# Down-projection weights loaded as one 16 KB run per partition, in a mixture-of-experts decoder kernel

## The chip, the core and the metric

The kernel runs on one core of a Trainium2 chip. The metric is the device time of one execution in microseconds (us). TensorE multiplies matrices (PE in the profile, its weight loads PEld), VectorE is DVE, ScalarE is ACT, GpSimd is POOL, and SyncE (SP) only issues DMA transfers here. SBUF is the memory on the chip with 128 partitions; HBM is the memory outside it.

## The reference, cut to what matters

Two decoder layers over 256 tokens of width 1024, all in fp32: in each an attention mixer with a residual add, then a mixture of experts with a residual add, and a final RMSNorm. The attention parts are not touched here. The expert part is, for each layer:

```
grp = top-1 of 4 groups;  top-2 of the 8 experts in that group       # per token
hid = silu(xb @ w_gate[e]) * (xb @ w_up[e])    # w_gate, w_up: 1024 x 512
y   = hid @ w_down[e]                          # w_down: 512 x 1024
out[token] += y * gate_weight
```

There are 32 experts in a layer. Each of the three matrices of an expert is 2 MiB, so the experts of one layer are 201 MB of weights, nearly all that the kernel reads.

## The kernel before, in words

The order of work is written out by hand for each engine, with semaphores between them. A layer is: projection of the attention inputs, attention, output product, routing, experts.

**Experts.** Every expert is computed for up to 32 of its tokens ("slots"). Experts go in groups of three (GE = 3): ten full groups, 0 to 9, and a tail group of two. For a full group TensorE does in turn:

- the gather of the tokens' rows by a product with a one-hot matrix (L835);
- for each of the three experts the gate and up product (L867): the 32 slots are the stationary operand, and the moving one is a piece of 128 gate columns and the same 128 up columns, so 256 columns for each of 8 chunks c of the inner dimension. The hidden dimension of 512 is cut into four pieces j. The pieces lie in four column strips of the array (tile_position), so the result stands in PSUM with piece j at rows 32j to 32j+31;
- the turn of the hidden values (L853), which gives hidT[k] with the place within the piece on the partitions and (piece, slot) along the row;
- keep_warm(6) (L736), products whose result nobody reads, issued after the wait for the second down block and ahead of the wait for the third;
- the down product (L887): for each piece j, the slots of piece j times row block j of the down weights;
- the scatter back to the tokens (L917), added to h by VectorE (L1301).

The profile shows each fp32 matmul as two instructions.

**The ring.** `ring` holds nine blocks of 16 KB per partition: gate and up of expert k at 2k and 2k+1, down at 6+k. Each is used once per group and filled again for the next group. SP issues all loads into one queue, in this order for a group: gate and up of expert k when the gate and up product of expert k of the group before is done (gate_up_done); then, when the down product of the group before is done (down_done), the three down blocks (load_down, L407). The tail group loads its last down block in two column halves (L429). For group 0 the loads are issued during and behind attention.

**Layouts.** Gate and up rows are spread so that partition p has rows 8p to 8p+7: one run of 16 KB in HBM. Down rows j*128+p are on partition p for j = 0 to 3: four runs of 4 KB. Row 128j+p of the down weights thus meets place p of piece j in hidT.

Of the kernel before, what the change touches and what calls it, by code (L numbers as in the profile page):

```python
# [1 line left out]

# [13 lines left out]
P = 128  # L36
# [28 lines left out]
HID = 512  # L65
# [121 lines left out]
def build(nc, x, mix_even, w_in_even, w_out_even, mix_odd, w_in_odd, w_out_odd, ffn_norm,  # L187
# [4 lines left out]
    with ExitStack() as ctx:  # L192
# [18 lines left out]
        ring = sb("ring", [P, 9, UNIT])  # L211
# [92 lines left out]
        e_arrived = [sems(f"e_arrived{l}_", 9) for l in range(LAYERS)]  # L304
# [82 lines left out]
        @block.sync  # L387
        def _(sp):
            gate_rows = w_gate.rearrange("l e (p c) n -> (l e) p (c n)", c=C)
            up_rows = w_up.rearrange("l e (p c) n -> (l e) p (c n)", c=C)  # L390
            down_rows = w_down.rearrange("l e (j p) n -> (l e) p j n", p=P)

            def load_group(l, r, g, experts, first_expert, after_attention=False):
                for k in range(experts):

                    if after_attention:
                        sp.wait_ge(proj_done[l], 2 * T * (k + 1))
                    else:
                        sp.wait_ge(gate_up_done[l], gu_count(r, g, k) - GE)
                    if after_attention and k == experts - 1:  # L400
                        load_w_out(l, 0)
                    row = l * EXPERTS + first_expert + k
                    sp.dma_start(ring[:, 2 * k, :], gate_rows[row]).then_inc(e_arrived[l][2 * k], 16)
                    sp.dma_start(ring[:, 2 * k + 1, :], up_rows[row]).then_inc(e_arrived[l][2 * k + 1], 16)
                def load_down(k):
                    row = l * EXPERTS + first_expert + k
                    sp.dma_start(ring[:, 6 + k, :].rearrange("p (j n) -> p j n", j=HID // P),  # L407
                                 down_rows[row]).then_inc(e_arrived[l][6 + k], 16)

                if after_attention:  # L410

                    sp.wait_ge(s_done[l], n_items[l])
                    load_w_out(l, 1)
                    load_down(2)
                    for k in range(2):
                        sp.wait_ge(mixed[l], T * (k + 1))
                        load_down(k)
                else:
                    sp.wait_ge(down_done[l], down_no(r, g))
                    for k in range(experts):  # L420
                        if experts == GE or k < experts - 1:
                            load_down(k)
                        else:

                            row = l * EXPERTS + first_expert + k
                            slot = ring[:, 6 + k, :].rearrange("p (j n) -> p j n", j=HID // P)
                            for half, arrived in ((0, e_arrived[l][6 + k]), (1, e_arrived[l][7 + k])):
                                cols = slice(512 * half, 512 * half + 512)
                                sp.dma_start(slot[:, :, cols], down_rows[row][:, :, cols]).then_inc(arrived, 16)  # L429

            def load_w_out(l, n):
                sp.dma_start(ring[:, 6 + n, :].rearrange("p (c n) -> p c n", c=C),
                             w_out[l][0].rearrange("(c p) n -> p c n", p=P)[:, :, 512 * n:512 * n + 512])\
                  .then_inc(w_arrived[6 + n], 16)

            def load_round(l, r, after_attention=False):
                if after_attention:
                    load_group(l, r, 0, GE, 0, after_attention)
                with sp.Fori(int(after_attention), FULL) as g:
                    load_group(l, r, g, GE, g * GE)  # L440
                load_group(l, r, FULL, TAIL, FULL * GE)

            for t in range(T):
                sp.dma_start(h[:, t, :], x[0, P * t:P * t + P, :]).then_inc(x_loaded[t], 16)
            sp.dma_start(cst[:, 0:FIRST_CONSTS], consts[:, 0:FIRST_CONSTS]).then_inc(const_loaded[0], 16)

            def load_gain(i, g):
                sp.dma_start(gains[:, i, :], g.rearrange("(p c) -> p c", c=C)).then_inc(gain_loaded[i], 16)

            load_gain(0, mix[0][0])  # L450
            more = None
            for l in range(LAYERS):
                w_in_v = w_in[l][0].rearrange("(p c) n -> p c n", c=C)
                for j in range(NW):
                    if l:

                        sp.wait_ge(gate_up_done[l - 1],
                                   gu_count(more, FULL, j // 2))
                    b = BLOCKS[l][j]
                    block, source = ring[:, j, :].rearrange("p (c n) -> p c n", c=C), w_in_v[:, :, 512 * b:512 * b + 512]  # L460
                    if j == 0:

                        sp.dma_start(block[:, 0:C // 2, :], source[:, 0:C // 2, :]).then_inc(w_begun, 16)
                        sp.dma_start(block[:, C // 2:, :], source[:, C // 2:, :]).then_inc(w_arrived[j], 16)
                        if l == 0:
                            for i, g in ((1, ffn_norm[0]), (2, mix[1][0]), (3, ffn_norm[1])):
                                load_gain(i, g)
                    else:
                        sp.dma_start(block, source).then_inc(w_arrived[j], 16)
                    if l == 0 and j == 2:  # L470
                        sp.dma_start(cst[:, FIRST_CONSTS:], consts[:, FIRST_CONSTS:]).then_inc(const_loaded[1], 16)
                if l == 0:
                    for m in range(LAYERS):
                        for dst, src in ((w_rt[:, m, :, 0:GROUPS], w_group[m].rearrange("(p c) e -> p c e", c=C)),
                                         (w_rt[:, m, :, GROUPS:], w_fine[m].rearrange("(p c) e -> p c e", c=C)),
                                         (b_rt[:, m, 0:GROUPS], b_group[m].partition_broadcast(P)),
                                         (b_rt[:, m, GROUPS:], b_fine[m].partition_broadcast(P))):
                            sp.dma_start(dst, src).then_inc(router_loaded, 16)
                load_round(l, 0, after_attention=True)
                sp.wait_ge(rounds_ready[l], 1)  # L480
                more = sp.value_load(rounds_i[0:1, l:l + 1], min_val=0, max_val=MAX_ROUNDS - 1)
                with sp.If(more > 0):
                    with sp.Fori(1, more + 1) as r:
                        load_round(l, r)

            for t in range(T):
                sp.wait_ge(xn_ready, T * LAYERS + t + 1)
                sp.dma_start(out[0, P * t:P * t + P, :], xn_t[:, t, :]).then_inc(out_stored, 16)
            sp.wait_ge(out_stored, T * 16)
# [242 lines left out]
        def _(pe):  # L732
# [80 lines left out]
            def values(l, a):  # L813
# [11 lines left out]
                                         start=(kt == 0), stop=(kt == T - 1), tile_position=(0, lo))  # L825
                last.then_inc(pair_done[l], 1)

            def experts_of(l, r, g, n):
                no = group_no(r, g)
                rows = SLOTS * n  # L830
# [24 lines left out]
                for k in range(n):  # L855
                    e = expert_no(r, g, k)
                    if k >= 2:
                        pe.wait_ge(gate_up_out[l], e - 1)
                    pe.wait_ge(e_arrived[l][2 * k], arrivals(2 * k, r, g))
                    pe.wait_ge(e_arrived[l][2 * k + 1], arrivals(2 * k + 1, r, g))  # L860
                    bank = psum[2 + k % 2]

                    for c in range(C):
                        if k == 0 and c == C // 2:
                            pe.wait_ge(xT_ready[l], no * 2 + 2)
                        for j in range(4):
                            last = pe.matmul(  # L867
                                bank[32 * j:32 * j + 32, 0:2 * P].rearrange("p (a s) -> p a s", a=2),
                                xT[:, c, SLOTS * k:SLOTS * k + SLOTS],
                                ring[:, 2 * k:2 * k + 2, 512 * c + P * j:512 * c + P * j + P],  # L870
                                start=(c == 0), stop=(c == C - 1), tile_position=(0, 32 * j))

                    last.then_inc(gate_up_done[l], 1 if n == GE or k < n - 1 else 1 + GE - n)
                    if k:
                        turn_hid(k - 1)
# [544 lines left out]
```

## Time and profile before

| | before |
|---|---|
| three runs, us | 1230.98, 1231.55, 1232.72 |
| median, us | 1231.55 |
| span of the profiled execution, us | 1232.3 |
| granted TensorE clock, mean | 0.925 |
| TensorE busy | 1022.5 us (83%) |
| VectorE busy | 421.3 us (34%) |
| ScalarE busy | 208.8 us (17%) |
| DMA, mean over the span | 358 GB/s, 441.25 MB |

The span is that of the one profiled execution, from its first to its last instruction. The page gives no other time of that execution; the span lies within the range of the three runs, so what lies around it is too small to be seen here. Busy time is the share of the span in which an engine has work; TensorE's includes keep_warm.

### The profile page before, as it was taken

The page shows a single profiled execution, that of the slowest core. Times are in us where ns is not written, and L with a number is a line of the kernel's source. Part 1 is how long each engine was busy: PE and PEld are TensorE (multiplying, and loading weights), DVE is VectorE, ACT ScalarE, POOL GpSimd, SP SyncE. Part 2 cuts the span into 40 slices and gives each one's busy share as a digit, 9 for nine tenths or more (in the row PEclk, how much of TensorE's full clock was granted, in tenths as well). Part 3 has the DMA queues.
Part 4 walks back from the last instruction along what each step waited for, and adds up shares of the span by engine and source line. Part 5 has one row for each costly group of instructions (what it writes and reads, how often), then busy time and mean ns, then how long its engine had stood idle before and what let it go on. Part 6 is the DMA issues. An engine that isn't in the chain of part 4 may idle for free.

```text
span 1232.3 us, 18607 instructions
## 1 busy us (share of the span) xinstructions
PE 1022.5 (83%) x7588; PEld 562.9 (46%) x7588; DVE 421.3 (34%) x1031; ACT 208.8 (17%) x531; POOL 36.6 (3%) x52
## 2 busy tenths in 40 slices
PE   8998988797787787787799999896977887877786
PEld 6874534442442442443378656344434433433442
DVE  5774522321321221222278735323212212221313
ACT  5643110100000000000155630001000000000101
POOL 1002000000000000000010210000000000000000
PEclk9999999998998898898889998999988998997988
DMA  9856389999999999999945543999999999999992
GB/s 358 285 212 266 137 343 419 418 430 418 418 427 423 419 423 424 419 421 421 362 165 239 225 168 124 376 419 416 428 422 420 423 425 419 421 426 420 419 421 106
DMA packets 76307, 441.25 MB, mean 358 GB/s; under 512 B 8816, under 2 KB 8816, under 8 KB 59760
## 3 DMA queue, kind: packets, MB, share of 16 engines
q1 hardware_dynamic: 76128, 440.26, 87.6%
q10 hardware_dynamic: 144, 0.52, 0.1%
q8 instruction: 22, 0.36, 0.1%
q14 instruction: 13, 0.11, 0.0%
HBM read 439.72 MB, written 1.05 MB: 358 GB/s over the span
## 4 chain that ended last, share of the span: by engine, by line
PE 51%; DMA 39%; DVE 6%; ACT 2%; issue 1%; SPq 1%; POOL 1%; DVEq 0%; ACTq 0%; POOLq 0%
DMA ring<-in_w_expert_down 38%; PE bank L736 12%; PE bank L887 11%; PE bank L867 5%; PE bank L924 4%; PE bank L759 3%; PE bank L761 3%; PE bank L760 3%; PE bank L835 2%; PE bank L917 2%; PE bank L898 1%; PE bank L957 1%; DMA ring<-in_w_in_even 1%; PE bank L810 1%; DVE work L1098 1%
## 5 line engine op out<-in xcount | busy, mean ns | idle before, releaser
L867 PE MATMUL bank<-ring,work 128*32 128x256 f32 x4096 | 249.6, 403 | 43.6 <-DMA ring<-in_w_expert_up 43.2
L867 PEld LDWEIGHTS bank<-ring,work 128*32 128x32 f32 x4096 | 141.8, 116 | 138.9 <-issue 67.6
L736 PE MATMUL bank<-cst 128*128 128x512 f32 x252 | 156.6, 785 | 42.1 <-DMA ring<-in_w_expert_down 42.1
L887 PE MATMUL bank<-ring,work 128*32 128x512 f32 x960 | 141.3, 594 | 0.0
L1296 DVE COPY work<-bank 96x512 f32<-96x512 f32 (+1 forms) x22 | 15.1, 687 | 350.6 <-PE bank L887 337.5
L736 PEld LDWEIGHTS bank<-cst 128*128 128x128 f32 x252 | 62.0, 256 | 119.3 <-issue 119.3
L835 PE MATMUL bank<-work,xn 128*128 128x96 f32 (+1 forms) x704 | 88.6, 287 | 22.9 <-DVE work L1264 22.9
L835 PEld LDWEIGHTS bank<-work,xn 128*128 128x128 f32 x704 | 84.9, 201 | 41.2 <-DVE work L1264 41.2
L917 PE MATMUL bank<-work 96*128 96x512 f32 (+1 forms) x176 | 85.1, 615 | 15.7 <-ACT work L620 15.7
L1290 DVE TENSOR_SCALAR work<-work 128x128 f32<-128x128 f32 x64 | 14.5, 226 | 224.5 <-ACT work L615 224.5
L887 PEld LDWEIGHTS bank<-ring,work 128*32 128x32 f32 x960 | 37.5, 110 | 100.8 <-issue 100.8
L759 PE MATMUL bank<-split,h_high 128*128 128x512 f32 x192 | 78.7, 410 | 5.6 <-DVE split L1089 4.0
L1089 DVE SCALAR_TENSOR_TENSOR split<-ring,gains,split 128x512 fp32r<-128x512 f32 x96 | 68.3, 749 | 27.9 <-ACT split L644 27.0
L760 PE MATMUL bank<-split,h_low 128*128 128x512 f32 x192 | 76.0, 396 | 0.0
L761 PE MATMUL bank<-split,h_high 128*128 128x512 f32 x192 | 76.0, 396 | 0.0
L1301 DVE TENSOR_TENSOR h<-h,bank 128x512 f32<-128x512 f32 x88 | 60.5, 687 | 39.8 <-PE bank L917 39.8
L644 ACT ACTIVATE split<-ring,gains 128x512 fp32r<-128x512 f32 x96 | 65.9, 720 | 31.4 <-PE bank L761 30.2
L620 ACT COPY work<-bank 96x512 f32<-96x512 f32 (+1 forms) x22 | 12.8, 582 | 331.8 <-PE bank L887 323.4
L853 PE MATMUL bank<-cst,work 128*128 128x128 f32 x64 | 21.4, 335 | 50.5 <-DVE work L1293 50.5
L614 ACT ACTIVATE work<-bank 128x128 f32<-128x128 f32 x64 | 17.7, 277 | 262.9 <-PE bank L867 262.9
L917 PEld LDWEIGHTS bank<-work 96*128 96x128 f32 (+1 forms) x176 | 28.1, 188 | 74.3 <-issue 47.1
L1291 DVE RECIPROCAL work<-work 128x128 f32<-128x128 f32 x64 | 61.0, 953 | 2.2
(145 smaller groups left out, 781.9 us busy)
## 6 DMA issues: line engine op xcount, KB each, us to landing
ring<-in_w_expert_gate SPq DMA_DIRECT2D x64, 2048.0 KB, 26.4
ring<-in_w_expert_up SPq DMA_DIRECT2D x64, 2048.0 KB, 30.1
ring<-in_w_expert_down SPq DMA_DIRECT2D x62, 2048.0 KB, 27.6
ring<-in_w_in_even SPq DMA_DIRECT2D x5, 2048.0 KB, 18.0
ring<-in_w_in_odd SPq DMA_DIRECT2D x5, 2048.0 KB, 20.9
ring<-in_w_out_even SPq DMA_DIRECT2D x2, 2048.0 KB, 8.3
ring<-in_w_expert_down SPq DMA_DIRECT2D x4, 1024.0 KB, 18.2
ring<-in_w_out_odd SPq DMA_DIRECT2D x2, 2048.0 KB, 8.4
```

What stands on the lines that cost most here:

```text
L644: act.activation(w_high[u % PARTS], ring[:, j, 512 * c:512 * c + 512], ACT.Copy, scale=gains[:, 2 * l, c:c + 1]).then_inc(w_high_ready, 1)
L736: pe.matmul(psum[7][:, :], data[:, 0:P], data, start=True, stop=True)
L759: pe.matmul(bank, high, wh, start=(c == 0), stop=False)
L760: pe.matmul(bank, low, wh, start=False, stop=False)
L761: last = pe.matmul(bank, high, wl, start=False, stop=(c == C - 1))
L835: last = pe.matmul(psum[c // 4][:, rows * (c % 4):rows * (c % 4) + rows], xn_c[:, t, c, :], onehot[:, t, 0:n, :].rearrange("p k s -> p (k ...
L867: last = pe.matmul(bank[32 * j:32 * j + 32, 0:2 * P].rearrange("p (a s) -> p a s", a=2), xT[:, c, SLOTS * k:SLOTS * k + SLOTS], ring[:, 2 ...
L887: last = pe.matmul(psum[6 + half][32 * k:32 * k + 32, :], hidT[k][:, 32 * j:32 * j + 32], ring[:, 6 + k, D * j + 512 * half:D * j + 512 * ...
L917: pe.matmul(psum[q % 2][:, :], gatedT[0:y_rows(n), P * t:P * t + P], y_sb[0:y_rows(n), 512 * half:512 * half + 512], start=True, stop=True)\
L1089: dve.scalar_tensor_tensor(out=w_low[u % PARTS], in0=ring[:, j, 512 * c:512 * c + 512], scalar=gains[:, 2 * l, c:c + 1], in1=w_high[u % PA ...
L1291: chain.link(dve.reciprocal(eb, eb))
L1301: dve.tensor_tensor(hv, hv, psum[q % 2][:, :], ALU.add).then_inc(added[l], 1)
```

## The change

A down block is loaded with rows 4p to 4p+3 on partition p, which is one run of 16 KB. So that hidT still meets its rows, piece j of the hidden dimension is no longer columns 128j to 128j+127 but the columns 4q+j for q = 0 to 127: the moving operand of the gate and up product takes every fourth column of the ring. The down product, the turn and all else are untouched. The halves of the tail's last down block follow the new rows too; their runs are 2 KB before and after.

```diff
-            down_rows = w_down.rearrange("l e (j p) n -> (l e) p j n", p=P)
+            down_rows = w_down.rearrange("l e (p j) n -> (l e) p j n", p=P)
...
-                    sp.dma_start(ring[:, 6 + k, :].rearrange("p (j n) -> p j n", j=HID // P),
-                                 down_rows[row]).then_inc(e_arrived[l][6 + k], 16)
+                    sp.dma_start(ring[:, 6 + k, :], down_rows[row].rearrange("p j n -> p (j n)"))\
+                      .then_inc(e_arrived[l][6 + k], 16)
...
+            def hidden_columns(k, c, j):
+
+                both = ring[:, 2 * k:2 * k + 2, 512 * c:512 * c + HID]
+                return both.rearrange("p a (q j) -> p a j q", j=HID // P)[:, :, j, :]
+
...
                             last = pe.matmul(
                                 bank[32 * j:32 * j + 32, 0:2 * P].rearrange("p (a s) -> p a s", a=2),
                                 xT[:, c, SLOTS * k:SLOTS * k + SLOTS],
-                                ring[:, 2 * k:2 * k + 2, 512 * c + P * j:512 * c + P * j + P],
+                                hidden_columns(k, c, j),
                                 start=(c == 0), stop=(c == C - 1), tile_position=(0, 32 * j))
```

## Rows read from the trace of the kernel before

**Rows 1.** The page: DMA share and GB/s in 40 slices, and packets.
```profile
DMA  9856389999999999999945543999999999999992
GB/s 358 285 212 266 137 343 419 418 430 418 418 427 423 419 423 424 419 421 421 362 165 239 225 168 124 376 419 416 428 422 420 423 425 419 421 426 420 419 421 106
DMA packets 76307, 441.25 MB, mean 358 GB/s; under 512 B 8816, under 2 KB 8816, under 8 KB 59760
```
**Rows 2.** The chain in order of time: start us, us, what.
```profile
150.61 3.81 PE bank L835 x32
154.64 7.04 PE bank L867 x128
161.94 3.63 PE bank L867 x64
...
187.97 3.81 PE bank L835 x32
...
220.16 27.01 DMA ring<-in_w_expert_down
247.31 7.17 PE bank L736 x12
...
381.48 8.35 PE bank L736 x12
...
560.37 7.65 PE bank L736 x12
...
575.80 3.88 PE bank L917 x8
...
587.93 9.23 PE bank L867 x128
...
764.48 3.81 PE bank L835 x32
...
800.15 3.81 PE bank L835 x32
...
1201.54 7.94 PE bank L867 x128
```
**Rows 3.** Who waited for whom: us in total, times, longest us.
```profile
PE bank L867 <- DMA ring<-in_w_expert_up: 43.2, 15, 3.6
PE bank L736 <- DMA ring<-in_w_expert_down: 42.1, 16, 3.7
```
**Rows 4.** SP's queue, 380 to 480 us; last, the page's issues.
```profile
422.93 1.18 SPq L404 DMA_DIRECT2D ring<-in_w_expert_up  x1
441.43 1.49 SPq L407 DMA_DIRECT2D ring<-in_w_expert_down  x3
...
ring<-in_w_expert_up SPq DMA_DIRECT2D x64, 2048.0 KB, 30.1
```
**Rows 5.** Windows: stretch, engines' busy us, clock, DMA share, GB/s.
```profile
278.50:291.50 13.00, 5.83 (x67) 3.00 (x66) 3.53 (x8) 1.50 (x7) 0.00 (x0) 0.87 1.00 401
295.50:308.50 13.00, 12.22 (x61) 3.81 (x59) 1.25 (x2) 0.58 (x1) 0.00 (x0) 1.00 1.01 430
...
502.10:515.10 13.00, 5.08 (x79) 2.89 (x71) 3.52 (x8) 1.69 (x7) 0.00 (x0) 0.95 1.01 406
...
532.10:545.10 13.00, 11.95 (x133) 7.58 (x135) 5.14 (x10) 0.91 (x3) 0.00 (x0) 1.00 1.02 432
```
**Rows 6.** Single lines: duration ns min/median/max, first and last start, forms.
```profile
L867 PE MATMUL bank<-ring,work x4096: 376/379/637, 154.6 to 1209.0; 128*32 128x256 f32 x196
...
L742 PEld LDWEIGHTS bank<-cst,h x64: 185/193/230, 6.8 to 753.5; 128*128 128x128 f32 x64
...
L736 PEld LDWEIGHTS bank<-cst x252: 186/192/338, 145.1 to 1180.9; 128*128 128x128 f32 x126
...
L1073 DVE TENSOR_SCALAR xn<-h,small x4: 1145/1148/1151, 133.9 to 760.6; 128x1024 f32<-128x1024 f32 x4
...
L1395 DVE SCALAR_TENSOR_TENSOR xn<-h,small,work x2: 1284/1284/1284, 1226.1 to 1227.9; 128x1024 f32<-128x1024 f32 x2
```

## The prediction

> **What bounds the kernel now.** I read the page first: the DMA line and the GB/s line by slices [rows 1]. In both expert phases (slices 7 to 19 and 27 to 39) the core's DMA engines are busy without a break at 416 to 430 GB/s; in the attention phases they are not. So the question is whether the weight stream or TensorE sets the pace of the experts, and the chain of waits in order of time answers it [rows 2]. Groups 0 and 1 of layer 0 run on weights that are already there: from gather to gather (L835) 187.97 - 150.61 = 37.36 us, all of it TensorE and the engines that it hands to. From group 2 on each step of the chain is a wait of 27 to 30 us for a down load, and keep_warm (L736), which stands behind the arrival of the second down block, starts at 247.31 in group 2 and at 560.37 in group 9: 313.06 us for 7 groups, 44.72 us each. A group loads 9 blocks of 2 MiB, 18.87 MB; over 44.72 us that is 422 GB/s, the rate of the page. TensorE has 44.72 - 37.36 = 7.4 us of room in a group; it shows as two waits, for the last up block and for the second down block, some 43 us each in the whole run [rows 3].
>
> Is the stream ever starved by TensorE, because SP issues a block's load only when its slot is free? In the steady group SP issues its last up load at 422.93, waits for the down product until 441.43 and only then issues the next three; but the median up load lands 30.1 us after its issue [rows 4], so some 10 us and more of the stream are still ahead when the new loads are put behind it. The queue never runs dry. While that holds, only bytes and the rate at which they move set the time of groups 2 to 9.
>
> **What the change does, part by part.** *The down load.* Gate and up blocks already come as one 16 KB run per partition; down comes as four of 4 KB. The windows view shows the rate while each kind flows [rows 5]: the queue's order is down, down, down, then three gate and up pairs, and the slow stretch returns every 44.7 us. Over six groups six windows of the down stretch have 401 to 406 GB/s (mean 404), and twelve of the gate and up stretch 427 to 434 (mean 429.4). A block of 2.097 MB takes 5.19 us at 404 and 4.88 us at 429.4: 0.31 us. Checked against the period: 3 x 5.19 + 6 x 4.88 = 44.9 us for a measured 44.72, so the windows are good to 0.4%. If all nine blocks moved at 429.4, the period would be 18.87 / 429.4 = 43.96, which is 0.76 us per group or 0.25 us per down block. I take 0.28, between 0.25 and 0.31, because with the change a down block has the same run length, size and destination as its neighbours at 429.4.
>
> How many down blocks count? The loads of group 0 come during and after attention and are hidden. From 158 us on the stream is unbroken (the first gate load of group 1 is issued when the first gate and up product of group 0 is done), so the three blocks of each of groups 1 to 8 count, and of group 9 the first two, because the chain leaves the stream at the arrival of the second; the third lands behind the keep_warm of 7.65 us. That is 26 blocks per layer. Behind that point (scatter, the tail group's gather, its products) the chain is TensorE's [rows 2], and both it and the loads of the tail group move forward together. The last block of the tail comes in two halves of 2 KB runs before and after: nothing. Sum: 2 x 26 x 0.28 = 14.6 us less; the ends 0.25 and 0.31 give 13.0 and 16.1.
>
> *SP's issue.* A down load has a quarter of the runs. SP gets through it no later than before, and what is queued behind (the next gate load) joins a stream that is never empty: nothing. If that cover were gone, SP's time would be a cost of before, not of after.
>
> *The gate and up product.* This is the part that could cost. L867 streams 256 columns of the moving operand per instruction; they were neighbours in the ring, and now lie 16 bytes apart. Instructions, columns, weights and bytes stay. Before, 128 instructions take 7.04 us, 55 ns each [rows 2], although one alone is recorded at 379 ns [rows 6]: the four column strips run side by side, each moving one column of 4 bytes in 7.04 us / 32 / 256 = 0.86 ns. No moving operand of the trace is read with such a step, so the cost is bounded by the nearest rows. From below: TensorE's weight load of h for L742 takes every eighth column, 32 bytes apart, and its median is 193 ns; that of a contiguous block in L736 is 192 ns. VectorE reads h with the same step in L1073 at 1148 ns per 1024 columns, 1.12 ns each; L1395 reads contiguous rows in 1284 ns [rows 6]. Both are single streams that fetch a new 16 bytes per element, about as fast as one strip does. So zero is the lower end; I see nothing by which the step could make it faster. From above: four strips at once take neighbouring columns 4 x 4 bytes per 0.86 ns, one group of 16 bytes per 0.86 ns; with the step of four they ask for four groups of 16 bytes in that time. If only one comes in that time, L867 becomes four times as long. No row excludes this, as no row has four strided streams. I take zero, by the rows nearest in step and engine, and keep the rest as rivals.
>
> A rule speaks against the change. The single-stream rows above show no price for a step of 32 bytes. The Trainium skill, "SBUF — State Buffer", section "Door 1: The DMA port swizzle", says that the memory works in lines of 16 bytes and that an access pattern needs two hits per line for full speed, so that every fourth fp32 column is where a penalty begins; it names no size. Taken as a doubling, it is the first rival below. In these rows the trace does not agree with it, but they are not the moving operand.
>
> What small slowdowns are worth: let L867 take a share x longer. In the groups bound by the stream it costs nothing until the 10.67 us of L867 per group (7.04 + 3.63) eat the room: 37.36 + 10.67x = 43.9 gives x = 0.61. Uncovered are the first expert of group 0, whose end starts the stream (3.5 us), and the tail's two experts (9.23 us in layer 0, 7.94 in layer 1 [rows 2]): 24.2x in all. It eats the gain of 14.6 at x = 0.60, almost where TensorE becomes the bound too. So below 0.6 the kernel is faster and above it slower.
>
> **The sum.** Span 1232.3 us; the three runs have 1230.98 to 1232.72, median 1231.55, so span and time agree to 0.1%. 1231.55 - 14.6 = 1217 us. TensorE's clock adds some noise: keep_warm in the chain takes 7.2 to 8.4 us [rows 2] by how much of it runs at half the clock; a change of 1 or 2 us in the last stream-bound group of each layer shifts the end. Its own range: 1211 to 1222.
>
> **Rivals.**
> *1. The stepped read doubles L867.* For it: one strip alone would fetch a line per column, and the four share a partition. Against it: the rows of single streams. Then a group takes 37.36 + 10.67 = 48.0 us, more than 43.96: TensorE is the bound in all ten groups. From 150.61 to the end of the scatter at 579.68 are 429 us; ten times 48.0 less the gap of 1 before the next gather are 479, +50, and the tail +9.2 and +7.9. With the shorter cycle of layer 1 (800.15 - 764.48 = 35.67, keep_warm at full clock) it is +33 per layer. Both layers: +84 to +118, so 1316 to 1350 us. It decides from x = 0.6.
> *2. It is four times as long*, by the bound from above. 37.36 + 32.0 = 69.4 (or 67.7) us per group: +247 to +263 per layer, and the tails +52: +546 to +578, about 1778 to 1810 us. For it: demand grows exactly fourfold. Against it: the full pace of L867 now, beside a running stream of 430 GB/s and busy VectorE, does not look like a port at its limit.
> *3. A part of it*, x from 0.1 to 0.6: 1219 to 1232 us.
> *4. The rate does not rise*, because the down blocks are slow for where they lie in HBM or for what TensorE reads beside them, not for their runs: 1229 to 1233 us. Against it: both kinds come from equal tensors and the rate changes with the kind in each of six groups. The gate and up stretches show 427 to 434 GB/s [rows 5]. The Trainium skill, "DMA: Bandwidth & Descriptors", section "Where 436 GB/s comes from", holds that the HBM side, about 358 GB/s per core, binds such loads; by it both kinds would be at one limit and nothing would be won. The trace does not agree.
>
> **Chances.** No cost in TensorE and the full gain 0.54; rival 1 0.18; rival 2 0.15; rival 3 0.08; rival 4 0.05. A measurement of this kernel tells about 0.2% (2.5 us) from no change. Faster: 0.54, half of rival 3 and 0.02 of rival 4, 0.60. Same: 0.05. Slower: 0.18 + 0.15 and 0.02 of rival 3, 0.35. The predicted time is that of the likeliest case, 1217. The range from 1211 to 1352 takes in rivals 1, 3 and 4 and leaves rival 2 out.
>
> **What would show it.** In the profile after: the packets under 8 KB fall by 62 x 512 = 31,744 from 59,760 [rows 1]; all windows at about 429 GB/s; keep_warm to keep_warm 43.9 to 44.0 us; L867 still 7.04 us per 128 and 379 ns; the two DMA waits of TensorE a little shorter. The prediction is wrong if L867's 128 instructions take over 11 us (rivals 1 and 2; then the waits for the ring go and the DMA line has gaps), or if the period stays at 44.7 with 16 KB packets (rival 4).

## The result and the profile after

The changed kernel takes 1337.05 us (median of 4 runs, 1336.18 to 1341.48) against 1232.13 us for the kernel before measured beside it: 1.0856 times as long, 95% interval 1.0836 to 1.0876. The prediction was 1217 us and faster. In every run on record the time lies 2.2 to 2.3 us above the span of the same execution; so the span of 1232.3 us before belongs to an execution of some 1234.5 us, and what lies around a span is not too small to be seen, as was said ahead of the prediction. Below, spans are compared with spans and times with times. In the listing after the change the lines have other numbers: the gather L835 is now L820, the gate and up product L867 is L852, keep_warm L736 is L716, the down product L887 is L872, the scatter L917 is L902.

The page of the kernel after, by slices, its packets, the shares of the chain that ended last, two groups and the up loads; it answers to [rows 1] and the last of [rows 4]:

```profile
PEclk9999999999999999999999998999999999999999
DMA  9855399999999999996834444999999999999960
GB/s 359 311 237 192 121 402 395 389 401 398 387 401 388 395 388 402 399 388 270 306 141 196 190 190 153 404 395 387 406 396 388 380 409 398 385 402 396 390 260 34
DMA packets 52498, 441.24 MB, mean 331 GB/s; under 512 B 8816, under 2 KB 8816, under 8 KB 28016
...
PE 85%; DVE 8%; ACT 3%; issue 2%; DMA 1%; POOL 1%; DVEq 0%; SPq 0%; ACTq 0%; POOLq 0%
...
L852 PE MATMUL bank<-ring,work 128*32 128x256 f32 x4096 | 474.6, 634 | 0.0
...
L716 PE MATMUL bank<-cst 128*128 128x512 f32 x252 | 130.3, 671 | 0.0
...
ring<-in_w_expert_up SPq DMA_DIRECT2D x64, 2048.0 KB, 14.6
```

The load did what it was to do: packets under 8 KB fell from 59,760 by exactly 31,744. But the expert phases now run at 380 to 409 GB/s, below before, and an up block lands 14.6 us after its issue in place of 30.1: the queue is nearly empty when SP issues, so it is no longer what the kernel waits for. TensorE waits for no DMA in L852 or L716 (idle before them: 0.0 each), and the DMA share of the chain is 1%. L852 is busy 474.6 us; L867 was 249.6.

The chain in order of time, one group of layer 0 and the gathers of the next two; it answers to [rows 2]:

```profile
197.72 3.81 PE bank L820 x32
201.75 14.79 PE bank L852 x125
...
216.79 7.49 PE bank L852 x59
...
227.13 5.16 PE bank L716 x12
232.29 7.03 PE bank L872 x48
...
244.98 3.81 PE bank L820 x32
...
293.52 3.81 PE bank L820 x32
```

Two experts' gate and up products take 14.8 us instead of 7.04, the third 7.5 instead of 3.63. These two groups are 47.3 and 48.5 us from gather to gather, as keep_warm falls into full (5.16 us) or partly half clock (6.5 us); over the whole of layer 0 a group is 47.1 to 48.9 us. Before it was 44.72, set by the stream. Windows of 13 us in the same part of the run as those of [rows 5] show the stream with gaps: a DMA share of 0.87 and 0.92 in two of the three, 1.00 in the other. In the first, SP had issued three down blocks at 287.88, which are 14.7 us of stream at 429 GB/s, and issues the next gate load only at 305.11, when TensorE has freed its slot; from 304 to 307 us the core moves 115 GB/s.

```profile
295.50:308.50 13.00, 13.00 (x119) 5.54 (x121) 2.88 (x6) 0.91 (x3) 0.00 (x0) 1.00 0.87 343
308.50:321.50 13.00, 11.67 (x102) 3.51 (x90) 2.68 (x6) 1.42 (x6) 0.00 (x0) 1.00 1.00 429
...
519.10:532.10 13.00, 11.53 (x58) 3.15 (x56) 3.40 (x6) 0.58 (x1) 0.00 (x0) 1.00 0.92 362
```

TensorE's timeline at the tail groups of both layers (start us, us, line and operation):

```profile
628.54 3.79 PE L820 MATMUL bank<-work,xn 128*128 128x64 f32 x32 [1.49 <-DVE work L1249]
...
632.48 14.86 PE L852 MATMUL bank<-ring,work 128*32 128x256 f32 x128
...
655.47 3.95 PE L902 MATMUL bank<-work 128*128 128x512 f32 x8
...
1294.23 3.79 PE L820 MATMUL bank<-work,xn 128*128 128x64 f32 x32 [1.61 <-DVE work L1249]
...
1321.04 3.95 PE L902 MATMUL bank<-work 128*128 128x512 f32 x8
```

With these the whole loss can be counted. Layer 0, first gather (148.97) to tail gather: 628.54 - 148.97 = 479.57 us, before 581.15 - 150.61 = 430.54: +49.0. Layer 1: 1294.23 - 814.64 = 479.59, before 1195.14 - 764.48 = 430.66: +48.9. The tail groups, from gather to the end of the scatter: 30.9 and 30.8 us, before 28.05 and 28.04: +2.8 and +2.7. Together 103.4 us. The first gather came 1.6 us earlier than before (148.97, 150.61), and 103.4 - 1.6 = 101.8 us is the difference in span, 1334.1 - 1232.3.

### The profile page after: what moved, and what is told of

It is laid out like the page before. It is cut to its first block, busy times and chain, and to the rows that moved or that the text cites. A ratio compares the mean times of both kernels' runs of the same rounds, so it can differ in the third digit from the quotient of the medians.

```text
span 1334.1 us, 18607 instructions
## 1 busy us (share of the span) xinstructions
PE 1211.0 (91%) x7588; PEld 566.0 (42%) x7588; DVE 421.3 (32%) x1031; ACT 208.9 (16%) x531; POOL 36.6 (3%) x52
## 4 chain that ended last, share of the span: by engine, by line
PE 85%; DVE 8%; ACT 3%; issue 2%; DMA 1%; POOL 1%; DVEq 0%; SPq 0%; ACTq 0%; POOLq 0%
PE bank L852 35%; PE bank L872 11%; PE bank L716 9%; PE bank L902 6%; PE bank L820 6%; PE bank L909 4%; PE bank L739 3%; PE bank L741 3%; PE bank L740 3%; DVE work L1276 2%; PE bank L838 1%; ACT work L600 1%; PE bank L883 1%; PE bank L942 1%; DVE work L1249 1%
## 5 line engine op out<-in xcount | busy, mean ns | idle before, releaser
L852 PE MATMUL bank<-ring,work 128*32 128x256 f32 x4096 | 474.6, 634 | 0.0
L852 PEld LDWEIGHTS bank<-ring,work 128*32 128x32 f32 x4096 | 160.7, 127 | 280.1 <-issue 277.7
L1275 DVE TENSOR_SCALAR work<-work 128x128 f32<-128x128 f32 x64 | 14.6, 227 | 404.4 <-ACT work L595 404.4
L872 PE MATMUL bank<-ring,work 128*32 128x512 f32 x960 | 141.3, 594 | 0.0
L716 PE MATMUL bank<-cst 128*128 128x512 f32 x252 | 130.3, 671 | 0.0
L820 PE MATMUL bank<-work,xn 128*128 128x96 f32 (+1 forms) x704 | 83.8, 277 | 23.0 <-DVE work L1249 23.0
L902 PE MATMUL bank<-work 96*128 96x512 f32 (+1 forms) x176 | 85.1, 615 | 15.7 <-ACT work L600 15.7
L820 PEld LDWEIGHTS bank<-work,xn 128*128 128x128 f32 x704 | 80.3, 192 | 41.2 <-DVE work L1249 41.2
L872 PEld LDWEIGHTS bank<-ring,work 128*32 128x32 f32 x960 | 37.5, 110 | 100.8 <-issue 100.8
L716 PEld LDWEIGHTS bank<-cst 128*128 128x128 f32 x252 | 53.2, 220 | 58.8 <-issue 58.8
L902 PEld LDWEIGHTS bank<-work 96*128 96x128 f32 (+1 forms) x176 | 28.1, 188 | 74.3 <-issue 47.1
L909 PE MATMUL bank<-ring,hT 128*128 128x512 f32 x128 | 57.1, 596 | 0.0
## 6 DMA issues: line engine op xcount, KB each, us to landing
ring<-in_w_expert_gate SPq DMA_DIRECT2D x64, 2048.0 KB, 10.2
ring<-in_w_expert_up SPq DMA_DIRECT2D x64, 2048.0 KB, 14.6
```

What stands on the lines that cost most here:

```text
L716: pe.matmul(psum[7][:, :], data[:, 0:P], data, start=True, stop=True)
L820: last = pe.matmul(psum[c // 4][:, rows * (c % 4):rows * (c % 4) + rows], xn_c[:, t, c, :], onehot[:, t, 0:n, :].rearrange("p k s -> p (k ...
L852: last = pe.matmul(bank[32 * j:32 * j + 32, 0:2 * P].rearrange("p (a s) -> p a s", a=2), xT[:, c, SLOTS * k:SLOTS * k + SLOTS], hidden_col ...
L872: last = pe.matmul(psum[6 + half][32 * k:32 * k + 32, :], hidT[k][:, 32 * j:32 * j + 32], ring[:, 6 + k, D * j + 512 * half:D * j + 512 * ...
L902: pe.matmul(psum[q % 2][:, :], gatedT[0:y_rows(n), P * t:P * t + P], y_sb[0:y_rows(n), 512 * half:512 * half + 512], start=True, stop=True)\
L909: last = pe.matmul(mix_bank(n, t)[:, :], oT[:, c, P * t:P * t + P], ring[:, 6 + n, 512 * c:512 * c + 512], start=(c == MIX_ORDER[l][0]), s ...
```

## The experiments

Two theories stood at the start. A: all of the loss is the stepped read of TensorE's moving operand, and the load by itself gives what was predicted for it. B: the load is (also) at fault. Under A a second question: does each moving stream pay for its step, or do only four strips together run out of supply?

### The load alone, and the step alone

```diff
-                                hidden_columns(k, c, j),
+                                ring[:, 2 * k:2 * k + 2, 512 * c + P * j:512 * c + P * j + P],
```

> Down blocks in 16 KB runs as in the change, but the gate and up product reads neighbouring columns as before. The hidden values then meet the wrong down rows, so the output is not the reference's; the work is the same. Theory: the whole loss sits in the stepped read, and the load by itself gives the 13 to 16 us of the prediction: 1216 to 1219 us, keep_warm to keep_warm about 43.9 us, windows of one rate near 429 GB/s. Rival: the load gives nothing (the down blocks were slow for another reason): 1229 to 1234 us and 44.7 us per group.

Measured: 1220.09 us, 0.9913 of before (0.9883 to 0.9943), which is 10.7 us less (7 to 14). Its page and two steps of its chain:

```profile
GB/s 356 303 206 275 139 303 429 429 427 428 428 429 429 427 430 427 429 428 428 391 200 233 223 167 129 371 429 428 429 428 428 428 427 430 428 429 428 428 428 112
```

```profile
261.55 29.01 DMA ring<-in_w_expert_down
...
526.88 28.11 DMA ring<-in_w_expert_down
```

All expert slices lie at 427 to 430 GB/s. The second down block lands at 290.56 in group 3 and at 554.99 six groups later: 44.07 us per group, before 44.72 [rows 2]. Theory A holds for the load, with a little less than it asked for: the time lies 1 us above the 1216 to 1219 us expected, and the interval of the gain, 7 to 14 us, takes in only the lower part of the 13 to 16 us.

```diff
-                    sp.dma_start(ring[:, 6 + k, :], down_rows[row].rearrange("p j n -> p (j n)"))\
-                      .then_inc(e_arrived[l][6 + k], 16)
+                    sp.dma_start(ring[:, 6 + k, :].rearrange("p (j n) -> p j n", j=HID // P),
+                                 down_rows[row]).then_inc(e_arrived[l][6 + k], 16)
```

(with down_rows as before; the product keeps its step.)

> The stepped read of the change alone, with the down blocks loaded as before (output not the reference's, same work). Theory: TensorE sets the pace of all ten groups, so the load no longer matters: 1335 to 1340 us, 128 instructions of the gate and up product in 14.7 us. Rival: the stepped read is only slow beside 16 KB writes into the ring: then this is near 1232 us with 7.04 us per 128.

Measured: 1340.96 us, 1.0896 of before (1.0852 to 1.0939), the same as the whole change within the intervals and 1 us above what was expected. Two experts' products take 14.85 us, so the rival, a step that costs only beside 16 KB writes, falls. The step alone makes the loss, and the faster load changes nothing under it.

### Which steps cost

The same kernel with old load and another step. Steps of two, three and eight columns in `hidden_columns`:

```diff
+                at = 512 * c + 256 * (j // 2)
+                both = ring[:, 2 * k:2 * k + 2, at:at + 256]
+                return both.rearrange("p a (q i) -> p a i q", i=2)[:, :, j % 2, :]
```

> As the run with the step alone, but the moving operand takes every second column (8 bytes apart, two per 16 bytes), piece j being columns 256*(j//2) + 2q + j%2 (output not the reference's). Theory 'two per line are enough': 7.04 us per 128 and 1232 us, as before. Theory 'cost grows with the bytes passed over': about half of the extra, 10 to 11 us per 128; a group then takes about 43 us in TensorE, still under 44.7, and the time is 1240 to 1246 us. Theory 'any step but one is slow': 14.7 us per 128 and 1337 us.

```diff
+                at = 512 * c + j
+                both = ring[:, 2 * k:2 * k + 2, at:at + 384]
+                return both.rearrange("p a (q i) -> p a i q", i=3)[:, :, 0, :]
```

> As the run with the step of four alone, but a step of three columns (12 bytes), columns 3q + j of each chunk (output not the reference's). If the cost follows the number of new 16-byte lines per column (0.75 for a step of three, 1 for four): 0.75 of the slow time, 11 us per 128 instructions. If it needs two hits in every line: near 14 us. If only a new line at every column costs: 7.04 us.

```diff
+                at = 1024 * (c // 2)
+                both = ring[:, 2 * k:2 * k + 2, at:at + 1024]
+                return both.rearrange("p a (q i) -> p a i q", i=8)[:, :, 4 * (c % 2) + j, :]
```

> As the run with the step of four alone, but a step of eight columns (32 bytes), over two neighbouring chunks (output not the reference's). If one new line per column is the whole cost: 14.7 us per 128 as with a step of four. If the cost goes on growing with the distance: 20 us and more, and the time above 1420 us.

TensorE's timeline of each at its first group of layer 0, in the order two, three, eight (the gate and up product is L852 or L853 in these listings):

```profile
154.33 7.48 PE L853 MATMUL bank<-ring,work 128*32 128x256 f32 x128
```

```profile
155.81 11.34 PE L853 MATMUL bank<-ring,work 128*32 128x256 f32 x128
```

```profile
155.81 14.96 PE L853 MATMUL bank<-ring,work 128*32 128x256 f32 x128
```

The same view of neighbouring columns (the kernel before) and of a step of four with the old load:

```profile
154.57 7.11 PE L867 MATMUL bank<-ring,work 128*32 128x256 f32 x128
```

```profile
156.96 14.85 PE L852 MATMUL bank<-ring,work 128*32 128x256 f32 x128
```

What orders these five numbers is how often a column falls into a new group of 16 bytes:

| step | new 16 bytes per column | us per 128 | ns per column |
|---|---|---|---|
| 1 | 0.25 | 7.11 | 0.87 |
| 2 | 0.5 | 7.48 | 0.91 |
| 3 | 0.75 | 11.34 | 1.38 |
| 4 | 1 | 14.85 | 1.81 |
| 8 | 1 | 14.96 | 1.83 |

(ns per column: the time over 32 rounds of four strips and 256 columns.) One price of 1.82 ns for each new 16 bytes gives 0.46, 0.91, 1.37, 1.82 and 1.82 ns; the first is covered by the 0.87 ns that a column takes anyway. So the cost neither starts with any step nor grows with distance; the theories "any step but one is slow" and "grows with the bytes passed over" fall, for fp32 and steps up to 32 bytes; nothing else was run. One run each: 1227.32 us for two and 1238.43 for three, where before had 1226.03 to 1235.75 and 1232.65. The run with a step of eight took 1855.02 us, above its expectation, but not by its pace: its values are wrong enough that routing in layer 1 asked for another round of experts (96 gate and up products in its trace, not 64; the 32 more all lie in layer 1). Only the pace is read from it, and from the runs below that leave pieces out with a step.

The Trainium skill, "SBUF — State Buffer", section "Door 1: The DMA port swizzle", has this as lines of 16 bytes of which each should be hit twice. The trace agrees: at two hits a line the product is 5% longer, at one hit 2.1 times as long. Its words on how far one can stride for free in fp32, 4 columns, are not borne out: a step of three already makes the product 1.6 times as long, a step of four 2.1 times.

### One stream or four

keep_warm of the kernel before with a stepped moving operand, one stream through the whole array:

```diff
+                data = cst[:, 0:2048].rearrange("p (q i) -> p i q", i=4)[:, 0, :]
+                for _ in range(n):
+                    pe.matmul(psum[7][:, :], cst[:, 0:P], data, start=True, stop=True)
```

> The kernel before, with keep_warm(6) of the expert groups reading every fourth column of the constants as its moving operand: one stream of 512 columns through the whole array, no strips beside it (the result of keep_warm is never read). Theory 'each stream pays for a new 16 bytes per column': the 12 instructions take about 10.3 to 11 us at the full clock in place of 5.16 (860 to 920 ns apiece). Theory 'only four strips together run out of supply': 5.2 us as before. The time stays near 1232 us by the room of 7.4 us per group, 1236 at most with the last group of each layer, if each stream pays.

```profile
168.26 10.96 PE L742 MATMUL bank<-cst 128*128 128x512 f32 x12
```

The contiguous 12 take 7.02 us at the same place in the kernel before. Each stream pays: 10.96 / 12 / 512 = 1.78 ns per column.

Both stretches lie partly at half clock: the granted clock is 0.84 over the stepped 12 and 0.76 over the contiguous ones. Over the run the contiguous 12 take from 5.16 us at full clock to 8.35 us at a clock of 0.64. The stepped 12 stay at 10.96 to 11.12 us with the clock between 0.85 and 0.76, and at 1.78 to 1.81 ns per column they have the pace that four strips have at a clock of 1.00. So the price of a new 16 bytes did not change with the granted clock, and a stepped product loses less beside a contiguous one where the clock is low.

The time, 1239.6 us (one run), lies above the 1236 expected. Its chain shows where the extra is:

```profile
560.38 11.11 PE bank L742 x12
```

This is keep_warm of group 9 in layer 0. It starts at 560.38, before at 560.37 [rows 2]: though the first three groups are 41.3 us each and not 37.36, the stream had hidden all of it by then. The stepped keep_warm then ends 3.5 us later, and 3.0 us later in layer 1 (11.12 us after 8.17); with +0.3 us in layer 1 up to there and -1.7 us in its tail group, whose other products run at a higher clock, that is the 5.0 us between the spans, 1237.3 and 1232.3. The expectation had about 2 us for the last group of a layer.

Fewer strips, with the step of four and old load:

```diff
-                        for j in range(4):
+                        for j in range(1):
```

> The step of four alone (old down load), with only piece j = 0 of the gate and up product computed; pieces 1 to 3 are left out, so one column strip streams at a time (output not the reference's). It has a quarter of the instructions, 32 per two experts. Theory 'four strips share the supply': each instruction now at the pace of contiguous data, about 0.22 us, 7.0 us for 32. Theory 'each stream pays': 0.46 us each, 14.7 us for 32, the same time as with four strips.

> As the run with one strip, with pieces 0 and 1 (64 instructions per two experts; pieces 2 and 3 left out). Shared supply of lines: between 7.0 and 14.7 us, by proportion 7.3 us (two strips ask for half of what four do). Each stream pays: 14.7 us again.

and the control, one strip on neighbouring columns:

> Control for the run with one strip: the kernel before with only piece j = 0 of the gate and up product, neighbouring columns; pieces 1 to 3 are left out. If a strip's pace does not depend on its neighbours, 32 instructions take 7.0 us, as 128 do with four strips; then the 14.6 us of the stepped single strip are its own cost, a factor of 2.1. If they take clearly less, part of the stepped cost came from something else.

TensorE's timeline of group 0, of one strip, two strips and the control:

```profile
157.27 14.62 PE L852 MATMUL bank<-ring,work 128*32 128x256 f32 x32
```

```profile
155.16 14.63 PE L852 MATMUL bank<-ring,work 128*32 128x256 f32 x64
```

```profile
152.95 7.09 PE L867 MATMUL bank<-ring,work 128*32 128x256 f32 x32
```

One, two and four strips have the same pace at a step of four, and one and four strips the same pace on neighbouring columns (7.09 and 7.11). The shared supply, on which the prediction's second rival rested, is refuted. (The runs with pieces left out and a step, 1888.79 and 1890.34 us, have an extra round of experts as above.)

### Does TensorE's length set the time?

The changed kernel without the keep_warm of the full groups:

```diff
-                        if k == n - 1:
-                            keep_warm(6, cst[:, 0:512])
```

> The changed kernel without the keep_warm products of the full expert groups (their result is never read). With the change a group takes about 47.7 us in TensorE, of which keep_warm is 5.2 to 6.9; without it about 42 us, less than the 43.9 us of the weight stream. Theory 'TensorE is the bound, and the room of 7.4 us was what counted': the stream sets the pace again, 1220 to 1240 us, the higher end if the clock falls in the waits. Rival: the extra time comes from loads issued late or slowed by the stepped reads, not from TensorE's own length: the time stays above 1300 us.

Measured: 1267.74 us, 1.0276 of before (1.0237 to 1.0315). From its chain:

```profile
195.82 3.81 PE bank L820 x32
199.85 14.79 PE bank L852 x125
...
225.68 8.79 PE bank L870 x48
...
240.12 3.81 PE bank L820 x32
```

and the window of that down product, with a granted clock of 0.80:

```profile
225.70:234.40 8.70, 8.70 (x48) 2.67 (x48) 0.00 (x0) 0.00 (x0) 0.00 (x0) 0.80 1.03 441
```

This group is 44.3 us, nine groups of layer 0 are 44.1 us on average, and 69 of the 105 us of loss are back. Late or slowed loads would not have given that, and TensorE waits for no DMA of weights in this run, so the rival falls. But the stream did not set the pace again, as the theory had expected (DMA has 0% of the chain): TensorE's 44.1 us are just what the stream needs too, 44.07 us in the run with the load alone. The expected time was too low for two reasons that the rows show. The down product mostly takes 8.8 us in place of 7.03, as it now meets half clock behind the pause for the hidden values. And I had set 43.9 us against the 44.72 of before for all groups, though groups 0 and 1 of a layer were 37.36 us before. By the trace the ten groups of layer 0 and of layer 1 are 10.2 and 9.0 us longer than before, the tail groups 5.5 and 4.9. The other 4.9 us of the 34.5 between the spans (1266.8, 1232.3) lie outside the expert groups and are not explained.

### Versions that keep the gain

Half way, with a step of two (free but for 5%) and two runs of 8 KB; the tail's last down block then comes in four loads instead of two:

```diff
-            down_rows = w_down.rearrange("l e (p j) n -> (l e) p j n", p=P)
+            down_rows = w_down.rearrange("l e (b p i) n -> (l e) p b i n", b=2, i=2)
...
+                    sp.dma_start(ring[:, 6 + k, :].rearrange("p (b m) -> p b m", b=2),
+                                 down_rows[row].rearrange("p b i n -> p b (i n)"))\
```

> A half way: a down block as two runs of 8 KB per partition (rows 256b + 2p and 2p + 1 on partition p), the gate and up product with a step of two columns; the output is the reference's. If a step of two is free and each run costs a fixed extra, two thirds of the gain of the full load remain: 8 to 11 us, 1221 to 1224 us. If a step of two costs, the kernel is slower than before, 1240 us or more.

Measured: 1227.75 us, 0.9954 (0.9936 to 0.9972), 5.7 us less (3 to 8), which is below the 8 to 11 us expected. Its chain has the second down blocks at 291.37 and 557.04:

```profile
262.34 29.03 DMA ring<-in_w_expert_down
...
528.30 28.74 DMA ring<-in_w_expert_down
```

That is 44.28 us per group, two thirds of the way from 44.72 to 44.07, so the share was right and the whole gain of which it was taken was too large. 52 down blocks at 0.15 us are 7.6 us, and 5% of L867 where nothing covers it take back 24.2 x 0.05 = 1.2 us: 6.4 us, within the interval. What the tail's four loads cost was not measured apart.

The full load, with the rows matched in VectorE's 32 x 32 turn; this takes the place of TensorE's turn and ScalarE's copy:

```diff
-                    dve.tensor_tensor(hid[k % 2], eb, gb[:, P:2 * P], ALU.mult).then_inc(hid_ready[l], 1)
+                    dve.tensor_tensor(hid[k % 2].rearrange("p (j r) -> p r j", j=4), eb.rearrange("p (r j) -> p r j", j=4),
+                                      gb[:, P:2 * P].rearrange("p (r j) -> p r j", j=4), ALU.mult).then_inc(hid_ready[l], 1)
+                    dve.wait_ge(hid_ready[l], e + 1)
+                    dve.transpose(hidT[k], hid[k % 2]).then_inc(hidT_ready[l], 1)
```

> Down blocks in 16 KB runs and the gate and up product on neighbouring columns; the rows are matched where the hidden values are turned: VectorE writes them with its columns grouped by j and turns 32 x 32 blocks, which puts hidden unit 4q+j of a piece on partition q, in place of TensorE's turn and ScalarE's copy. Output is the reference's. If the stepped read was the only fault of the change: 1214 to 1219 us, 43.9 us per group. Rival: VectorE's turn (128 x 128, perhaps 0.3 us or more) and its stepped writes make VectorE late; it has 34% load, so this would show as a wait of the down product for VectorE, and at most 1 us at the end of each layer.

Measured: 1216.6 us, 0.9867 (0.9838 to 0.9896), 16.4 us less than before (13 to 20), as expected. It beats both kernels. It gains more than the load alone did (7 to 14 us); the two intervals just touch, and what the new turn adds of its own was not measured apart. The turn's own line, the stepped write ahead of it and the same operation before; then TensorE's longest waits:

```profile
L1257 DVE STREAM_TRANSPOSE work<-work x64: 311/311/314, 163.8 to 1199.8; 128x128 f32<-128x128 f32 x64
```

```profile
L1254 DVE TENSOR_TENSOR work<-work x64: 374/380/389, 163.4 to 1199.4; 128x128 f32<-128x128 f32 x64
```

```profile
L1293 DVE TENSOR_TENSOR work<-work x64: 291/291/293, 160.4 to 1211.6; 128x128 f32<-128x128 f32 x64
```

```profile
PE bank L709 <- DMA ring<-in_w_expert_down: 94.1, 18, 6.1
PE bank L833 <- DMA ring<-in_w_expert_up: 45.7, 16, 3.7
```

The turn takes 0.31 us and the write with a step of 32 columns 0.38 us where the plain one took 0.29. TensorE's longest waits are for the stream, 94.1 us for down blocks after 42.1 [rows 3]: the 50.5 us that it used to wait for the hidden values before turning them (L853 for L1293 in the kernel before) are gone, and that room shows here. The down product of the full groups waits for VectorE nowhere, that of the tail groups 1.0 us in all.

## Why the prediction was wrong

**What bounds the kernel.** Right. With the step on, the room of 7.4 us per group was what counted. A step of three makes the product 58% longer (11.34 + 5.72 us for 10.77). With the old load the room ends at x = 7.36 / 10.67 = 0.69, and one run took 1238.43 us beside 1232.65: a small loss, with one wait for the stream left in the chain of layer 0, in group 9.

**The down load.** Right in mechanism, a little large in size: 0.22 us per block ((44.72 - 44.07) / 3) where 0.28 was taken and 0.25 was the lower end. 52 x 0.22 = 11.4 us, measured 10.7 (7 to 14). The 0.31 came from two rates of windows, which overstated the period by 0.2 us beside a difference of 0.9; and the stream reached 428.3 GB/s (18.87 MB in 44.07 us) and not 429.4.

**The gate and up product.** Here the prediction failed: "I take zero, by the rows nearest in step and engine". Those rows were TensorE's weight load at 193 ns with a step of 32 bytes and VectorE's read at 1.12 ns per column. Neither is the moving operand. The moving operand's price, 1.82 ns for each new 16 bytes, makes the product 2.1 times as long: 14.8 us for 128 instructions where 7.04 was put, 11.6 us more per group against a room of 7.4. The bound from above was wrong in its reason: the four strips share nothing that the step exhausts.

The rows were also misread. L742 is a transpose, and it was held against L736, a plain product. The transposes of the same size that read neighbouring columns were in the trace of before:

```profile
L853 PEld LDWEIGHTS bank<-cst,work x64: 137/138/183, 161.6 to 1212.0; 128*128 128x128 f32 x64
```

```profile
L810 PEld LDWEIGHTS bank<-cst,work 128*128 128x128 f32 x72 | 8.1, 140 | 15.2 <-POOL work L539 14.1 <-issue 0.5
```

Their weight loads take 138 and 140 ns, that of L742, with every eighth column, 193 ns [rows 6]. So the nearest row, held against its like, is 40% longer with the step, though no run changed the step of a weight load alone. It is not the price of the moving operand, by which 128 columns would take 233 ns. VectorE's row says as little: L1395 has two tensors to read and L1073 one. Operations of its kind with neighbouring columns take 226 ns for 128 of them (L1290) and 286 ns for 256 (L1097), which would give some 650 ns for 1024, an estimate, where L1073 took 1148 ns. That the step makes this difference is not shown; that it costs nothing is not either.

**The rivals.** The first, "the stepped read doubles L867", is what happened: 1337 us, where it gave 1316 to 1350. It had a chance of 0.18. Its size of a group was right (48.0 us; measured 47.1 to 48.9 in layer 0). Two of its terms were off, and that the time fell into the middle of its range is partly luck: layer 1 does not run at the shorter cycle (+48.9 and not +33), as keep_warm is at full clock in some groups of either layer and not in others; and the tails cost +2.8 and +2.7, not +9.2 and +7.9. Their products had been partly at half clock before and are not any more: in layer 0 the gather takes 3.79 us after 6.35, and the gate and up products 14.86 us after 9.25. The second rival's 1778 to 1810 us is refuted with its reason, and the fourth by the windows at 429 GB/s and the run with the load alone.

**The rule that was set aside.** The 16-byte rule of the Trainium skill was at hand and was weighed against rows of other ports and another operation; I let them decide. The range held the time, by the width that rival 1 gave it; the forecast and the chance of 0.60 for faster did not hold.

## What to carry to other kernels

A layout that makes a DMA's runs longer moves the stride to whoever reads the tile. Before trusting that a strided read is free, find a row of the same port with the same step, and hold a stepped row only against the same operation without the step; here even the weight load of a transpose, 193 ns after 138, had the warning. In an fp32 moving operand keep two used columns in each 16 bytes, or put the permutation where it is cheap: here in a turn that had to be done anyway. And compare the cost with the room: it was the 7.4 us per group that made 11 us of longer products a loss of this size.

## What was not expected of the hardware

The price of a stepped moving operand is a clean function of new 16-byte groups: 1.8 ns each, the same in one, two or four column strips at full clock, and in a full-width product of 512 columns at a granted clock of 0.76 to 0.85. Other accesses with a step pay less: TensorE's weight load with every eighth column takes 193 ns for 128 columns where neighbouring ones take 138, and VectorE's product with a write step of 32 columns 380 ns after 291. Down runs of 4, 8 and 16 KB gave periods of 44.72, 44.28 and 44.07 us for the same bytes. Against 16 KB that is 0.65 us for three runs more per partition and 0.21 us for one more, which fits a fixed 0.22 us per group for each further run of its three down blocks.
